# Layer norms by a two-column root and a diagonal product

## The reference, cut to what matters

```
def layer_norm(x, g, b):
    mu = mean(x, -1)
    var = mean(square(x - mu), -1)
    return (x - mu) * rsqrt(var + LN_EPS) * g + b

x = layer_norm(ALPHA * x + (1 + g_m) * y, ln_mix_g[i], ln_mix_b[i])    # ln0, ln2
u = x * (1 + sc_f) + sh_f
x = layer_norm(ALPHA * x + (1 + g_f) * y, ln_ffn_g[i], ln_ffn_b[i])    # ln1, ln3
```

## Time and profile before

| | |
|---|---|
| runs, us | 3270.58, 3277.40, 3277.83; median 3277.4 |
| profiled execution, us | 3271.7 |
| its span, us | 3269.6 |
| granted TensorE clock, mean | 0.980 |
| TensorE (PE) busy | 3124.2 us, 96% |
| VectorE (DVE) busy | 1016.0 us, 31% |
| ScalarE (ACT) busy | 485.4 us, 15% |
| HBM | 224 GB/s over the span |

### The profile page before, as it was taken

The page is one execution under the profiler, slowest core; times in us unless marked ns, Lnnn a source line. Parts: engine busy times, 40 slices in busy tenths (PEclk is TensorE's granted clock), DMA queues, the critical chain, the costliest instruction groups (busy, mean ns, idle before and its releaser), DMA issues.

```text
span 3269.6 us, 56266 instructions
## 1 busy us (share of the span) xinstructions
PE 3124.2 (96%) x24052; PEld 2619.3 (80%) x24053; DVE 1016.0 (31%) x2245; ACT 485.4 (15%) x1106; POOL 15.6 (0%) x27
## 2 busy tenths in 40 slices
PE   5999999999999999999999989997889999999998
PEld 4888888888888888888888867877776688667875
DVE  5203332330230231424015554378431211121212
ACT  1001022110100101221001311015221011101111
POOL 0000000000000000000000000000000000000000
PEclk8999999999999999999999999998899999999999
DMA  8645634364374474436436436741257988889885
GB/s 340 263 167 208 242 133 185 141 246 180 126 294 172 164 283 161 181 129 225 178 151 248 179 117 251 296 188 77 101 217 273 358 330 314 314 312 356 339 309 208
DMA packets 55479, 732.27 MB, mean 224 GB/s; under 512 B 6608, under 2 KB 6792, under 8 KB 10804
## 3 DMA queue, kind: packets, MB, share of 16 engines
q1 hardware_dynamic: 51364, 716.68, 57.4%
q0 software_dynamic: 3984, 13.74, 1.2%
HBM read 729.31 MB, written 4.23 MB: 224 GB/s over the span
## 4 chain that ended last, share of the span: by engine, by line
PE 82%; DVE 8%; DMA 7%; issue 2%; ACT 1%; SPq 0%; DVEq 0%; ACTq 0%
PE psum L659 50%; PE psum L1102 12%; PE psum L1145 9%; PE psum L646 3%; PE psum L717 3%; DMA ring<-in_up_e_dram 2%; DMA ring<-in_up_dram 2%; DVE ring L1540 2%; DVE work L1526 1%; PE psum L1126 1%; PE psum L1161 1%; DMA ring<-in_w_v_dram 1%; DMA ring<-in_w_qk_dram 1%; PE psum L742 0%; PE psum L699 0%
## 5 line engine op out<-in xcount | busy, mean ns | idle before, releaser
L659 PE MATMUL psum<-h_t,ring 128*128 128x256 f32 x5888 | 1286.6, 381 | 12.9 <-DMA ring<-in_up_dram 6.4
L659 PEld LDWEIGHTS psum<-h_t,ring 128*128 128x128 f32 x5888 | 1118.9, 191 | 178.9 <-issue 22.6
L659 PE MATMUL psum<-work,ring 128*128 128x256 f32 x2752 | 599.9, 381 | 10.0 <-DVE x_t L2228 5.2
L659 PEld LDWEIGHTS psum<-work,ring 128*128 128x128 f32 x2752 | 524.0, 191 | 83.9 <-issue 11.6
L1102 PE MATMUL psum<-h_t,ring 128*64 128x96 f32 x11264 | 472.2, 246 | 6.5 <-DMA ring<-in_up_e_dram 6.5
L1102 PEld LDWEIGHTS psum<-h_t,ring 128*64 128x64 f32 x11264 | 468.7, 137 | 9.3 <-issue 7.9
L1145 PE MATMUL psum<-ring,work 128*96 128x512 f32 x704 | 304.1, 593 | 0.7 <-DMA ring<-in_down_e_dram 0.7
L1540 DVE SCALAR_TENSOR_TENSOR ring<-ring,cond 128x1024 f32<-128x1024 f32 x240 | 279.1, 1219 | 13.0 <-DMA ring<-in_ada_dram 12.5
L1145 PEld LDWEIGHTS psum<-ring,work 128*96 128x96 f32 x704 | 114.1, 163 | 184.9 <-issue 183.1
L1603 DVE TENSOR_TENSOR work<-work,psum 128x256 f32<-128x256 f32 (+1 forms) x118 | 49.7, 421 | 622.4 <-PE psum L659 607.4
L2421 DVE TENSOR_TENSOR work<-work,psum 128x256 f32 x176 | 74.1, 421 | 400.3 <-PE psum L1102 400.3
(11 more groups left out here) (349 smaller groups left out, 1532.6 us busy)
## 6 DMA issues: line engine op xcount, KB each, us to landing
ring<-in_up_e_dram SPq DMA_DIRECT2D x64, 2048.0 KB, 7.6
ring<-in_ada_dram SPq DMA_DIRECT2D x60, 2048.0 KB, 7.7
ring<-in_up_dram SPq DMA_DIRECT2D x55, 2048.0 KB, 8.1
ring<-in_down_e_dram SPq DMA_DIRECT2D x32, 1792.0 KB, 8.0
ring<-in_down_dram SPq DMA_DIRECT2D x20, 2816.0 KB, 9.6
ring<-in_up_e_dram SPq DMA_DIRECT2D x32, 1536.0 KB, 8.4
ring<-in_down_e_dram SPq DMA_DIRECT2D x16, 2048.0 KB, 8.0
ring<-in_w_qk_dram SPq DMA_DIRECT2D x12, 2048.0 KB, 8.6
```

The lines of the kernel that those rows point to most:

```text
L659: mm = pe.matmul(half(b), w, moving(k, j * lin.groups + m), start=(k == 0), stop=(k == depth - 1))
```

## The change

The sum of squares is made with the tokens on the partitions: for each tile k and each half t of the tokens, the squared data are the stationary operand and one column of ones is the moving one, so bank 6 gets two columns (token t*128 + p at partition p, column t). Scaling, root and reciprocal run on these two columns (`root_t`, 128x2). VectorE then multiplies the identity by them into `rms` (128 x (2 x 128), a diagonal matrix per half), and TensorE multiplies ones by it: every partition of bank 6 holds the row of 256 reciprocal roots. The first scaled tile reads this row from PSUM; behind it `spread_in` copies the row to `rms`, and the other tiles read it there. The wait for the centred tiles moves from `scaled` to ahead of the diagonal.

On ScalarE, `load_root_table`, a root of one column into an unused cell, stands ahead of the squares, so that the table is loaded there. In ln1 `inputs_in(0)` moves from ahead of the root to behind it. On TensorE the wait for the diagonal and the product stand in the queue behind the squares' products and, in ln1, ahead of the remaining S5 transposes.

```diff
--- before.py
+++ after.py
@@ -175,7 +175,7 @@
     up_rms = lambda src, adas: Linear(11, 4, 32 * P, src, adas, 1, biased=2)
     down = lambda src: Linear(4, 2, 44 * P, src)
     norm = with_(uses(b5=1), raw=DT, squares=DT, most_squares=1, root=1, scaled=DT, h=DT)
-    ln = with_(uses(b5=1, b6=1), mean=DT, squares=DT, root=1, h=DT)
+    ln = with_(uses(b5=1, b6=2), mean=DT, squares=DT, root=1, diagonal=1, h=DT)
     ln_fused = with_(ln, most_x=1, scaled=DT)
     logits = with_(uses(b4=2, b5=2, b6=2, b7=2), maxima=1, probs=HG, bias_in=16)
     mix = uses(b4=2, b5=2, b6=3, b7=3)
@@ -433,6 +433,7 @@
         mh = tiles(0, MT)
         ln_scale, ln_shift = small[:, 232:240], small[:, 240:248]
         x_scale, x_shift = lvec[:, 0:DT], lvec[:, DT:2 * DT]
+        root_t, table_cell = small[:, 250:252], small[:, 252:253]
         var_m, factor, centre = small[:, 56:64], small[:, 216:224], small[:, 224:232]
         by_head = lambda a: a.rearrange("p (t n) -> p t n", n=MH)
         extra = skip.rearrange("p f c -> p (f c)")
@@ -696,8 +697,13 @@
                 pe.wait_ge(bank_free[6], reads(p, 6))
                 for k in range(DT):
                     pe.wait_ge(signal["squares"], p.of("squares", k + 1))
-                    mm = pe.matmul(half(6), ones[:, :], h[:, k, :], start=(k == 0), stop=(k == DT - 1))
+                    for t in range(TT):
+                        mm = pe.matmul(half(6)[:, t:t + 1], h[:, k, t * P:(t + 1) * P], ones[:, 0:1],
+                                       start=(k == 0 and t == 0), stop=(k == DT - 1 and t == TT - 1))
                 mm.then_inc(signal["full6"], 1)
+                pe.wait_ge(signal["diagonal"], p.of("diagonal", 1))
+                pe.wait_ge(bank_free[6], reads(p, 6, 1))
+                pe.matmul(half(6), ones[:, :], rms[:, :], start=True, stop=True).then_inc(signal["full6"], 1)
 
             def ffn(up, down, ready=None, after=None, rms_of=None):
                 linear(up, lambda k, n: h[:, k, :], ready, rms_of=rms_of)
@@ -1242,14 +1248,24 @@
                     act.wait_ge(signal["scaled"], p.of("scaled", k + 1))
                     act.activation(h[:, k, :], h[:, k, :], ACT.Identity, bias=mod[:, k:k + 1]).then_inc(signal["h"], 1)
 
+            def load_root_table():
+
+                act.activation(table_cell, ones[:, 0:1], ACT.Sqrt).then_inc(act_done, steps.one())
+
+            def token_root(p):
+
+                act.wait_ge(bank_free[6], reads(p, 6, 0) + 1)
+                act.activation(root_t, root_t, ACT.Sqrt).then_inc(signal["root"], 1)
+
             def centred_squares(p):
                 for k in range(DT):
                     act.wait_ge(signal["mean"], p.of("mean", k + 1))
                     act.activation(h[:, k, :], x[:, k, :], ACT.Square).then_inc(signal["squares"], 1)
 
             def layer_norm(p):
+                load_root_table()
                 centred_squares(p)
-                root(p, 6)
+                token_root(p)
                 if "scaled" not in p.what:
                     return
                 for k in range(DT):
@@ -1443,10 +1459,10 @@
 
             kernels_in()
             magnitudes()
+            load_root_table()
             centred_squares(place("ln1"))
-            inputs_in(0)
-            root(place("ln1"), 6)
-            for g in range(1, 8):
+            token_root(place("ln1"))
+            for g in range(8):
                 inputs_in(g)
             p = place("s5")
             for half_of in range(2):
@@ -1742,14 +1758,29 @@
                 dve.wait_ge(bank_free[5], reads(p, 5, 0) + 1)
                 for k in range(DT):
                     dve.tensor_tensor(x[:, k, :], x[:, k, :], rms[:, :], ALU.subtract).then_inc(signal["mean"], 1)
-                mean_square(p, 6, LN_EPS)
+                dve.wait_ge(bank_full[6], products(p, 6))
+                dve.tensor_scalar(root_t, half(6)[:, 0:TT], 1.0 / D, LN_EPS, ALU.mult, ALU.add).then_inc(bank_free[6], 1)
+                dve.wait_ge(signal["root"], p.of("root", 1))
+                dve.reciprocal(root_t, root_t).then_inc(dve_done, steps.one())
+                dve.wait_ge(dve_done, steps.count())
+                dve.wait_ge(signal["mean"], p.of("mean", DT))
+                dve.tensor_tensor(rms[:, :].rearrange("p (t s) -> p t s", t=TT),
+                                  ident[:, :].unsqueeze(1).to_broadcast([P, TT, P]),
+                                  root_t.unsqueeze(2).to_broadcast([P, TT, P]), ALU.mult).then_inc(signal["diagonal"], 1)
+                dve.wait_ge(bank_full[6], products(p, 6, 1))
+
+            def spread_in(p):
+
+                dve.tensor_copy(rms[:, :], half(6)).then_inc(bank_free[6], 1)
+                dve.wait_ge(bank_free[6], reads(p, 6, 1) + 1)
 
             def scaled(p, o, g):
 
-                dve.wait_ge(signal["mean"], p.of("mean", DT))
                 for k in range(DT):
-                    dve.scalar_tensor_tensor(o[:, k, :], x[:, k, :], g[:, k:k + 1], rms[:, :],
+                    dve.scalar_tensor_tensor(o[:, k, :], x[:, k, :], g[:, k:k + 1], rms[:, :] if k else half(6),
                                              ALU.mult, ALU.mult).then_inc(signal["scaled"], 1)
+                    if k == 0:
+                        spread_in(p)
 
             def x_times():
 
@@ -2242,8 +2273,10 @@
             sp5 = place("s5")
             for half_of in range(2):
                 for k in range(4 * half_of, 4 * half_of + 4):
-                    dve.scalar_tensor_tensor(h[:, k, :], x[:, k, :], ln_scale[:, k:k + 1], rms[:, :],
+                    dve.scalar_tensor_tensor(h[:, k, :], x[:, k, :], ln_scale[:, k:k + 1], rms[:, :] if k else half(6),
                                              ALU.mult, ALU.mult).then_inc(dve_done, steps.one())
+                    if k == 0:
+                        spread_in(place("ln1"))
                 dve.wait_ge(dve_done, steps.count())
                 for k in range(4 * half_of, 4 * half_of + 4):
                     dve.tensor_scalar(h[:, k, :], h[:, k, :], ln_shift[:, k:k + 1], None, ALU.add).then_inc(signal["h"], 1)
```

## The result

Over 20 runs each, the changed kernel took 3287.22 us in the median (3271.09 to 3294.62) and the kernel before 3272.62 us (3265.72 to 3281.11): ratio 1.0039, with a 95% interval of 1.0029 to 1.0049, some 13 us (the medians themselves differ by 14.6). Forecast were 3276.5 us and a change of -0.8. The profiled execution took 3287.46 us (span 3285.1), against 3271.7 (3269.6).

What follows compares the result with a forecast made beforehand. The prediction took TensorE's long weight-streaming products to bound the kernel, layer norms counting only as holes between them. Its terms for ln0 to ln3, -0.4 + 0.36 - 0.4 - 0.33 = -0.77 us, gave 3276.5 us, range 3268 to 3282.

Steps and rivals of the forecast that it cites:

- I take 0: Each norm's squares' products: 32 one-column instructions take 3.65 us against 3.73, taken as 0, ends -0.1 and +0.2.
- The chain of 1.91 us: Each norm, from VectorE's first instruction on the sum to the first scaled tile: 1.91 us instead of 2.70.
- the allowance for the half clock: The diagonal's product: 0.71 us to VectorE's read, and some 0.2 to 0.4 more at the half clock.
- the 0.79: Each norm's shorter way from the sum: the first scaled tile comes 0.79 us earlier.
- The copy: Behind the first scaled tile: VectorE's copy takes 0.46 us, covered in ln0 and ln2, paid in ln1 and ln3.
- The early load: Table load ahead of the squares: nothing either way in ln0, ln2 and ln3; in ln1 squares start 1.06 us later.
- Forecast for ln1: VectorE is the bound behind ln1, and tiles after the first come later: +0.36 us, ends 0 and +0.7.
- the clock is full up to the first transposes: -0.33: ln3: TensorE's clock stays full and the copy is paid, so 0.33 us are gained.
- The -0.4 of ln0 and of ln2: TensorE starts 0.79 us sooner in ln0, but the time gained may run at half clock; ln2 alike: -0.4 us each.
- Rival B: One-column products drop TensorE's clock: +3.6 us each in ln0, ln1, ln3, +1.5 in up3; +11.6 in all, 3289; chance 0.05.
- the steady 0.111 us of the denominators' 24: Argument against a falling clock: the mLSTM denominators' 24 instructions kept a 0.111 us step to the end.
- other placing of clock stretches, code loading: 0.02: The remainder beside forecast and rivals: clock stretches placed otherwise, or code loading; chance 0.02.

Runs made afterwards that it cites:

- a_noload: The changed kernel without load_root_table, so the table load stands ahead of the root again: 3279.75 us, 1.0018 of the kernel before.
- a_pad: The changed kernel with 291 satisfied waits (146 slots) in TensorE's queue ahead of the expert loop: 3281.22 us, 1.0023 of the kernel before.
- a_fill: The changed kernel with one more 256-column product per squared tile, into the unused half of bank 6: 3292.58 us, 1.0057 of the kernel before.
- b_layout: The kernel before with 111 slots of satisfied waits ahead of the expert loop and 8 more in its body: 3279.73 us, ratio 1.0022.
- b_pad125: The kernel before with 249 satisfied waits (125 slots) in the S5 stage, ahead of the expert loop: 3272.79 us, ratio 0.9994.
- b_pad: The kernel before with 222 satisfied waits (111 slots) in TensorE's queue ahead of the expert loop: 3275.01 us, ratio 1.0002.

## Why the prediction was wrong

What the steps said, and what the runs showed:

- Squares' products, "I take 0": right at the full clock (3.70 us in ln1 of a_noload and a_pad, against 3.65 forecast and 3.69 before). Wrong in the clock, which falls during them in 31 of 36 norms (3.8 to 7.0 us) and stays down for what follows. This is the first failed step: the norms were to give 0.77 us and cost 6.0.
- The chain of 1.91 us: three steps within 0.01 us, the diagonal 0.10 shorter. Its product, taken at 0.71 from another one, took 0.74 at the full clock (a_fill, ln3) and 1.26 otherwise; the allowance for the half clock (0.2 to 0.4 more, measured 0.5) was named and not taken into the sum. With it the chain is 2.37 us in ln0: 0.33 us are left of the 0.79, before the copy's 0.46.
- The copy: 1986.49 to the next tile at 1986.94, 0.45 us, as forecast; off the path it changed nothing that could be measured.
- The early load: in ln1 ScalarE's piece ahead ends at 2238.80 and the squares start at 2240.22, 1.42 us behind it where it was 0.45: 0.97 later, forecast 1.06. At equal squares' products (3.70) ln1's stage was 24.4 to 25.0 us in four profiles with it and 23.35 in one without (a_noload); 0.35 of these 1.1 to 1.7 us is the diagonal's product, wholly at the half clock in the four. Forecast for ln1 was +0.36; measured +2.4, most of the rest being the clock. By the times of a_noload the load costs more than its norms show, some 7 us of the 13, and why stays open.
- ln3, "the clock is full up to the first transposes: -0.33": +1.5. Nine of nine one-column ln3 had slowed products. The earlier trace rows told of a norm with wide products, and the change takes just these away. The -0.4 of ln0 and of ln2 were +1.0 and +1.1, mostly for the same reason.
- Rival B had the mechanism and 0.05. Its argument against, the steady 0.111 us of the denominators' 24, was of one series in one execution. The series does take 2.73 or 2.74 us, at the full clock, in all 20 profiles. But in the changed kernel's first profile the fall came 1.4 us into ln1's products and 1.8 into ln3's, sooner than 2.7 us, so length alone isn't the difference. That series has 512-column products (line 893) directly ahead and behind, and the norm's has idle time behind it and mostly ahead; whether this decides is not shown. Rival B's price was too high: it had the whole series at half clock in three norms, +11.6; the norms gave +6.0.
- The rest, "other placing of clock stretches, code loading: 0.02": the second failed step. The working priced only edited stages, and put the experts' +7.8 us at nothing. The earlier trace rows even has "issue" with 2% of the chain, 65 us, and the kernel before has one stall of 6.5 us at this loop, so a cost of this kind was in sight. The split by runs is loose and does not add up: a_pad gives back 5 us of 13, a_noload 7, both 9, and b_layout alone costs 1 to 13.
- The early load brings no draining: the root's cell follows the load's end (2240.09) by 0.02 us, as the first trace had it. The 1.38 us of the Trainium skill, ScalarE: Activation LUTs (What ACT_TABLE_LOAD costs), don't show here either.

The range, 3268 to 3282, was the spread of three runs; 20 runs of the kernel before spread over 15 us and the changed kernel's over 24. What stays open: which property of the layout brings the second stall (equal start and sizes showed none in two profiles, yet a slower median), and what in a series of one-column products lets the clock fall in one execution of ln1 and not in another, and what the early load costs beyond ln1.

## What to carry to other kernels

32 instructions of one column took as long as the 16 of 256 that they replaced, but TensorE's clock fell in them far more often, and its work behind them then pays too (the diagonal's product 1.22 us instead of 0.70); a swap from wide to narrow products has to be priced at both clocks. Count the slots that an edit adds to a long loop's program and ahead of it, and look for "issue" waits at the loop's head before and after: with 119 slots more, the experts' stage lost 7.8 us in the mean of three profiles, where the norms lost 6.0. And take more than one profile of each: the loop's third pass, or one norm's clock, differs between executions of one program by as much as the edit is worth. Before a reciprocal is made cheap by moving it to other partitions, look whether the engine in front of it can give it directly; how exact that function is, no run here measures.

## What the hardware showed that was not expected

- TensorE's granted clock fell while the engine was busy without a hole (1.00 to 0.50 between 2241.8 and 2242.8 in ln1, 1.4 us after a hole of 0.84), with no transfers going on (DMA share 0.00).
- A loop whose body is some 1,900 slots waits, most likely for its instructions, at the head of the second pass, 6.0 to 7.4 us in every profile, and at the third in some executions of the same program: 7.19 us in one of b_pad125, whose other 11 runs are 14 us or more faster. In one profile of b_pad it was the fifth pass, 6.19 us; in no profile were there more than two such stalls.
- ScalarE's reciprocal root on 128x256 takes 0.42 us, where root and VectorE's reciprocal took 0.42 + 1.75.
